# Page numbers read ahead, three fill banks in the attention, and two passes of the last block moved into the linear attention

## What is computed

```python
def compress_blocks(rows, pe, w1, w2):            # rows: all tokens' K or V, past pages included
    blk = rows[:, :nb * 64].reshape(B, nb, 64, 2, G, D)
    h = jax.nn.silu(jnp.einsum('bnlcgd,lcde->bncge', blk + pe[:, :, None, :], w1))
    return jnp.einsum('bncge,cef->bncgf', h, w2)

def nsa(x, ...):                                  # prompt and sample group alike
    q, q_rot, cmp_kv, slc_kv, win_kv, gates = nsa_project(x, pos, w_in, b_gate)
    o_cmp, imp = cmp_attention(q, pos, compress_blocks(...))
    o_slc = sel_attention(q_rot, ..., select_blocks(imp, pos, nb_sel), slc_kv)
    o_win = win_attention(q_rot, ..., win_kv)
    return (gates[0] * o_cmp + gates[1] * o_slc + gates[2] * o_win) @ w_out

def gla(x, s0, ...):                              # chunks of 32 tokens
    o = att @ v + q_i @ S;  S = a_last * S + k_s.T @ v
    return (rms_norm(o) * norm_g * silu(r)) @ w_out

y = layer_norm(ALPHA * y + mixer(y));  y = layer_norm(ALPHA * y + swiglu(y))
```

## Time and profile before

| | |
|---|---|
| time, median of 3 runs | 1784.22 us (1784.01 to 1786.27) |
| the profiled execution: its own time | 1787.92 us |
| its span, first to last instruction | 1786.2 us |
| TensorE matmul busy | 1644.1 us, 92% |
| TensorE weight load busy | 1496.4 us, 84% |
| DVE, ACT, POOL busy | 595.9, 577.5, 722.5 us |
| mean granted TensorE clock | 0.954 |
| phase_compress | about 177 to 325 us |
| attention, stretch with `keys` and `scores` | about 350 to 489 us |
| phase_gla ends, t1 begins | 1331.65 us |

### The profile page before, as it was taken

The page is one execution under the profiler, slowest core; times in us unless marked ns, Lnnn a source line. Parts: engine busy times, 40 slices in busy tenths (PEclk is TensorE's granted clock), DMA queues, the critical chain, the costliest instruction groups (busy, mean ns, idle before and its releaser), DMA issues. The chain is left out here.

```text
span 1786.2 us, 37763 instructions
## 1 busy us (share of the span) xinstructions
PE 1644.1 (92%) x14970; PEld 1496.4 (84%) x14970; DVE 595.9 (33%) x1212; ACT 577.5 (32%) x1142; POOL 722.5 (40%) x503
## 2 busy tenths in 40 slices
PE   6998789688989978999999998998979999999997
PEld 6998677465666678999999998987659999999996
DVE  2111010545555638211111138127547411111114
ACT  3221000255454525422322224226434532222313
POOL 6640321343344556644344327403126644334320
PEclk9998898699999989999999999999979999999998
DMA  7326885254535643433333213324214233323201
GB/s 209 104 81 164 253 269 183 74 160 145 156 113 173 180 130 118 144 116 118 108 117 93 85 48 95 86 70 144 81 60 130 86 116 95 89 86 99 86 22 48
DMA packets 297287, 211.56 MB, mean 118 GB/s; under 512 B 34148, under 2 KB 290328, under 8 KB 296600
## 3 DMA queue, kind: packets, MB, share of 16 engines
q1 hardware_dynamic: 279000, 175.69, 33.1%
q0 software_dynamic: 7552, 20.06, 3.6%
q10 hardware_dynamic: 10560, 13.41, 2.7%
HBM read 199.02 MB, written 18.42 MB: 122 GB/s over the span
## 5 line engine op out<-in xcount | busy, mean ns | idle before, releaser
L1582 POOL TENSOR_TENSOR w_low_t<-w_raw,w_high_t 128x1024 fp32r<-128x1024 f32 (+1 forms) x130 | 307.0, 2370 | 336.8 <-ACT w_high_t L1685 336.8
L1665 PE MATMUL ps<-x_high,w_high_t 128*128 128x256 f32 (+1 forms) x1488 | 425.4, 286 | 8.3 <-POOL w_low_t L1582 5.9
L1667 PE MATMUL ps<-x_high,w_low_t 128*128 128x256 f32 (+1 forms) x1488 | 421.6, 283 | 0.0
L1666 PE MATMUL ps<-x_low,w_high_t 128*128 128x256 f32 (+1 forms) x1488 | 420.9, 283 | 0.0
L1665 PEld LDWEIGHTS ps<-x_high,w_high_t 128*128 128x128 f32 x1488 | 281.9, 189 | 10.6 <-POOL w_low_t L1582 6.2
L1666 PEld LDWEIGHTS ps<-x_low,w_high_t 128*128 128x128 f32 x1488 | 282.2, 190 | 0.3
L1667 PEld LDWEIGHTS ps<-x_high,w_low_t 128*128 128x128 f32 x1488 | 282.1, 190 | 0.0
L1685 ACT CAST w_high_t<-w_raw 128x1024 fp32r<-128x1024 f32 (+1 forms) x130 | 132.0, 1024 | 154.3 <-PE ps L1667 126.1
L1807 DVE TENSOR_TENSOR h_t<-silu_t,ps 128x256 f32<-128x256 f32 (+1 forms) x88 | 37.4, 425 | 366.2 <-PE ps L1667 359.7
L1665 PE MATMUL ps<-hid_high,w_high_t 128*128 128x264 f32 (+1 forms) x542 | 153.6, 283 | 0.0
L1667 PE MATMUL ps<-hid_high,w_low_t 128*128 128x264 f32 (+1 forms) x542 | 153.2, 283 | 0.0
(11 more groups left out here) (367 smaller groups left out, 3208.2 us busy)
## 6 DMA issues: line engine op xcount, KB each, us to landing
w_raw<-in_ffn_w_gu SPq DMA_DIRECT2D x88, 512.0 KB, 3.8
pages<-in_cache_slc SPq DMA_DIRECT2D x192, 128.0 KB
rows<-in_cache_cmp SPq DMA_DIRECT2D x123, 128.0 KB, 3.7
w_raw<-in_ffn_w_down SPq DMA_DIRECT2D x32, 448.0 KB, 3.5
w_raw<-in_gla_w_in SPq DMA_DIRECT2D x24, 512.0 KB, 3.8
rows<-in_cache_cmp ACTq DMA_DIRECT2D x70, 128.0 KB, 4.9
pages<-in_cache_slc POOLq DMA_DIRECT2D x64, 128.0 KB, 2.8
w_raw<-in_ffn_w_down SPq DMA_DIRECT2D x16, 512.0 KB, 3.7
```

Of the source, the lines that this page charges most:

```text
L1582: nc.gpsimd.tensor_tensor(low(u)[:, 0:k], raw[:, u % RAW, 0:k], high(u)[:, 0:k].bitcast(F32), ALU.subtract).then_inc(low_done, 1)
L1665: nc.tensor.matmul(psum(i), high(u)[:, k, :], a[0][:, at, c], start=(k == 0), stop=False)
L1666: nc.tensor.matmul(psum(i), high(u)[:, k, :], a[1][:, at, c], start=False, stop=False)
L1667: ins = nc.tensor.matmul(psum(i), low(u)[:, k, :], a[0][:, at, c], start=False, stop=(k == t.kc - 1))
```

## The change

Three edits, without a change to what is computed or to the number of matmuls, copies or transfers.

1. **Page numbers.** A helper `row_pages` reads a queue's page numbers of a unit; the numbers of unit 1 are read in phase_project (SP: ahead of issuing the new caches; ACT: behind the `w1` loads; GpSimd: at its end). In phase_compress `load_part` only waits and issues, and `read_ahead` reads the numbers of the next unit behind it. ACT's `load_part` for unit n+2 now stands ahead of the sigmoid of unit n, with the wait for the buffer. SP's nine tables move behind the loads of unit 2 (six) and unit 3 (three). The two loads of position rows now stand behind GpSimd's reads for unit 5.
2. **Fill banks.** In the first part of the attention (the first 182 of the 366 steps, 116 of the 190 fills) the fills go round three banks, 4, 6 and 5. The outputs of `pv` move to columns 384 to 511 of bank 7, beside the sample scores. A `pv` of an even unit waits until DVE has taken all scores before it (`sc_out`), a `scores` step until DVE has taken out all finished pairs (`o_done`), and DVE takes a pair out at the next `qk` or `scores` step. `scores` steps that fell between an even `pv` and its odd one are moved behind the odd one: 8 of 20 move, and some groups of `keys` with them. From step 182 on all is as before.
3. **Passes.** The first two passes of t1 (units 0 and 1, tokens 0 to 255) are made inside phase_gla, one behind the last `kv`, one behind the last `o`, in banks 2 and 3, which `kv` has left. t1 begins with its third pass.

```diff
+def row_pages(eng, S, n, by):
+    p = n % (NB * PAGES // ROW_UNIT)
+    return [eng.value_load(S["pt"][0:1, p * ROW_UNIT + m:p * ROW_UNIT + m + 1], min_val=0, max_val=N_POOL - 1)
+            for m in range(ROW_SHARE[by], ROW_SHARE[by + 1])]
...
             for m in range(LATE):
                 first_page(sp, m)
+            S["next_pages"][0] = row_pages(sp, S, 1, 0)
...
         def load_part(eng, n, by, arrived):
-            c, p = UN[n]
-            lo, hi = SHARE[by], SHARE[by + 1]
-            pages = [eng.value_load(pt[0:1, p * QP + m:p * QP + m + 1], min_val=0, max_val=N_POOL - 1)
-                     for m in range(lo, hi)]
             if n >= 2:
                 eng.wait_ge(conv_done, n - 1)
-            for m, page in zip(range(lo, hi), pages):
+            for m, page in zip(range(SHARE[by], SHARE[by + 1]), S["next_pages"][by]):
...
+        def read_ahead(eng, n, by):
+            if n < len(UN):
+                S["next_pages"][by] = row_pages(eng, S, n, by)
...
         def _(pool):
             for n, (c, p) in enumerate(UN):
                 if n:
                     load_part(pool, n, 2, rows_sw)
+                    read_ahead(pool, n + 1, 2)
                 if n and p == 0:
...
         def _(act):
+            load_part(act, 1, 1, rows_act)
             for c in range(2):
                 act.dma_start(w2[64 * c:64 * c + 64], io["nsa_w_cmp2"][0, c]).then_inc(w2_in, 16)
-            load_part(act, 1, 1, rows_act)
+            read_ahead(act, 2, 1)
...
+                if n + 2 < len(UN):
+                    load_part(act, n + 2, 1, rows_act)
                 act.wait_ge(pre_done, n + 1)
                 if n >= 1:
                     act.wait_ge(hid_done, n)
                 nc.scalar.activation(sig[own, :, 0:k], pre[own, :, 0:k], ACT.Sigmoid).then_inc(sig_done, 1)
-                if n + 2 < len(UN):
-                    load_part(act, n + 2, 1, rows_act)
+                read_ahead(act, n + 3, 1)
...
+    dealt, ORDER, held, pair_open = ORDER, [], [], False
+    for step in dealt:
+        if step[0] == "scores" and pair_open or held and step[0] == "keys" and step[1] >= held[0][1] + 2:
+            held.append(step)
+            continue
+        ORDER.append(step)
+        if step[0] == "pv":
+            pair_open = UN[step[1]][2] == 0
+            if not pair_open:
+                ORDER += held
+                held = []
...
+    SLOT = [f % 3 if f < FILLS3 else (f - FILLS3) % 2 for f in range(len(FILL))]
+    TURN_OF = [SLOT[0:f + 1].count(SLOT[f]) for f in range(len(FILL))]
...
-        SCORE, OUT, SAMPLE = (0, 2), 5, 7
-        BANK = (4, 6)
+        SCORE, SAMPLE = (0, 2), 7
+        BANK = (4, 6, 5)
+        def out_of(n):
+            return ps[:, SAMPLE, 384:384 + P] if n in NEAR else ps[:, BANK[2], 0:P]
...
+                if n in NEAR:
+                    pe.wait_ge(own_masked, 1)
+                    if SCORES_TO["pv", n, 0]:
+                        pe.wait_ge(sc_out, SCORES_TO["pv", n, 0])
+                elif ORDER[SWITCH] == ("pv", n, 0):
+                    pe.wait_ge(fill_out[2], SLOT.count(2))
...
+                if PAIRS_TO["scores", i, 0]:
+                    pe.wait_ge(o_done, PAIRS_TO["scores", i, 0])
...
         def psum(i):
-            return ps[:, i % STAT, 0:width(passes[i][1])]
+            return ps[:, (i + begun) % STAT, 0:width(passes[i][1])]
...
+                if i < begun:
+                    continue
...
         ORDER.append(("kv", 2 * t + 1))
+        if t == TILES - 1:
+            ORDER.append(("next", 0))
...
+    ORDER.append(("next", 1))
     ORDER += [("rec", TILES - 1), ("norm", TILES - 1), ("oT", TILES - 1), ("gate", TILES - 1)]
...
+            def next_pass(u):
+                pe.wait_ge(cst["pre_low"]["t1"], u + 1)
+                pe.wait_ge(xh_done, 2)
+                pe.wait_ge(xl_done, 3)
+                pe.wait_ge(st_done, 8 * (len(KV) - 1) + 2 * (u + 1))
...
+                ins.then_inc(cst["pre_mm"], 1)
```

More of the change, by code:

```diff
@@ L934, in phase_attention @@
     ORDER += [x[:3] for x in sample[at_s:]]
-    FILL = {step: f for f, step in enumerate(x for x in ORDER if x[0] in ("turn", "keys", "probs", "back"))}
+    dealt, ORDER, held, pair_open = ORDER, [], [], False
[9 more added lines that the diff above has]
+                held = []
+    FILL = {step: f for f, step in enumerate(x for x in ORDER if x[0] in ("turn", "keys", "probs", "back"))}
+    LAST_SCORES = max(at for at, x in enumerate(ORDER) if x[0] == "scores")
+    SWITCH = next(at for at, x in enumerate(ORDER) if at > LAST_SCORES and x[0] == "pv" and UN[x[1]][2] == 0)
+    NEAR = {x[1] for at, x in enumerate(ORDER) if at < SWITCH and x[0] == "pv"}
+    FILLS3 = sum(x in FILL for x in ORDER[0:SWITCH])
+    SLOT = [f % 3 if f < FILLS3 else (f - FILLS3) % 2 for f in range(len(FILL))]
+    TURN_OF = [SLOT[0:f + 1].count(SLOT[f]) for f in range(len(FILL))]
+    SCORES_TO = {x: sum(y[0] == "scores" for y in ORDER[0:at]) for at, x in enumerate(ORDER) if x[0] == "pv"}
+    PAIRS_TO = {x: sum(y[0] == "pv" and UN[y[1]][2] == 1 for y in ORDER[0:at])
+                for at, x in enumerate(ORDER) if x[0] == "scores"}
+    WHOLE_AT = {}
+    for at, x in enumerate(ORDER):
+        if x[0] == "pv" and UN[x[1]][2] == 1:
+            WHOLE_AT[next(y for y in ORDER[at:] if y[0] in ("qk", "scores"))] = x[1]
     def by_act(step):
@@ L963, in phase_attention @@
                              "scaled4", "pv_done4", "o_done4"))
-        fill_done, fill_out = sem("fill_done"), [sem("fill_out%d" % b) for b in range(2)]
+        fill_done, fill_out = sem("fill_done"), [sem("fill_out%d" % b) for b in range(3)]
         ring = S["ring"]
@@ L1077, in pv @@
                     for a in range(2):
-                        nc.tensor.matmul(ps[own(a), OUT, 0:P], S["vb"][:, split_heads(p, a), :], S["pT"][:, t, :],
+                        nc.tensor.matmul(out[own(a)], S["vb"][:, split_heads(p, a), :], S["pT"][:, t, :],
                                          start=True, stop=False, tile_position=(0, 64 * a))
@@ L1083, in pv @@
                         c = (2 * (p // R) + a) * D
-                        ins = nc.tensor.matmul(ps[own(a), OUT, 0:P], v[:, k, c:c + D], pT[:, n % 2, a * (t + 1) + k, :],
+                        ins = nc.tensor.matmul(out[own(a)], v[:, k, c:c + D], pT[:, n % 2, a * (t + 1) + k, :],
                                                start=False, stop=(br == 1 and k == t), tile_position=(0, 64 * a))
@@ L1363, in _ @@
                 kind, n, f = step
-                if kind == "qk" and n > VLAG and UN[n - VLAG - 1][2] == 1:
-                    out_whole(n - VLAG - 1)
+                if step in WHOLE_AT:
+                    out_whole(WHOLE_AT[step])
                 if kind == "qk" and n < U:
@@ L1458, in load_unit, with phase_trunk @@
         sp.dma_start(raw[:, u % RAW, 0:t.kc], t.W[:, t.k0:t.k0 + t.kc, t.col:t.col + P]).then_inc(w_in[u % RAW], 16)
-def phase_trunk(nc, io, ps, cst, name, xT, X, H, stages, bounds, store, early=0, cast=0, moved=None, then=None):
+def phase_trunk(nc, io, ps, cst, name, xT, X, H, stages, bounds, store, early=0, cast=0, begun=0, moved=None, then=None):
     walk = Walk(stages, bounds)
@@ L1648, in _ @@
                     turn((i - first_half - 3) // 2)
-                if hf == 0:
+                if i < begun:
+                    continue
+                if hf == 0 or (u, 0) in passes[0:begun]:
                     split(pe, u)
@@ L2235, in turn_sample @@
                 ins.then_inc(fill_done, 1)
+            def next_pass(u):
[3 more added lines that the diff above has]
+                pe.wait_ge(st_done, 8 * (len(KV) - 1) + 2 * (u + 1))
+                c = slice(*SPLIT[0])
+                out = ps[:, BEGUN + u, 0:c.stop]
+                for kk in range(KT):
+                    nc.tensor.matmul(out, cst["w_high"][:, u, kk, :], X[0][:, kk, c], start=(kk == 0), stop=False)
+                    nc.tensor.matmul(out, cst["w_high"][:, u, kk, :], X[1][:, kk, c], start=False, stop=False)
+                    ins = nc.tensor.matmul(out, cst["w_low"][:, u, kk, :], X[0][:, kk, c], start=False, stop=(kk == KT - 1))
+                ins.then_inc(cst["pre_mm"], 1)
             for kind, n in ORDER:
@@ L2239, in _ @@
                     project(n)
+                elif kind == "next":
+                    next_pass(n)
                 elif kind == "low":
```

63 lines of the change are left out of this document (39 added, 24 removed).

## The result

The changed kernel takes 1774.1 us (median of 4 runs, 1770.45 to 1775.33), the one before 1784.95 us beside it (4 runs, 1784.01 to 1786.27): a ratio of 0.9936, 95% interval 0.9924 to 0.9949, or 10.9 us less. The forecast was 1771, 13.2 less. Of the three terms behind it one came out at less than half, one at two to three times its size.

A forecast was written before the change was run, and what follows sets the result against it. TensorE was taken to wait for late pages in phase_compress, bank copies in the attention and a chain ending phase_gla. Terms -10.4 - 2.3 - 0.5 = -13.2 us, from 1784.22 to 1771 us; range 1758 to 1779.

The forecast's parts named there:

- Rival A: phase_compress: transfers are the bound, later gaps stay, unit 1 gains 6.8, unit 4 pays 2.3; total 1777 us, chance 0.16.
- Edit 1, -10.4 forecast: phase_compress: pages issued earlier shrink the gaps ahead of units to 9.5 us, 10.4 us faster; ends -16 and -2.
- Pages are there at 194.3 instead of 201.09: phase_compress, unit 1: 4.2 MB at 317 GB/s take 13.2 us from 181.1, leaving a gap of 2.2 of 9.03 us.
- The covers: Reads for unit 1 in phase_project cost nothing, up to 7.5 us otherwise; DVE's product behind ACT's sigmoid is due a unit later.
- The cost of unit 4: phase_compress: position rows issued behind nine reads land last, so a gap of 2.3 us stands where 1.96 was.
- Edit 2, -2.3 forecast: Attention's keys stretch: third bank gains 10.5 us, new stalls cost 8.2, so 2.3 us faster; ends -11 and +3.
- The sum of the cost: Attention: nine scores waits of 0.8 us, 7.2, plus 1 us for even pv waits: 8.2 us.
- of 12.0 us I leave 1.5: Attention: a third bank covers TensorE's bank waits of up to about 1.2 us, a gain of 10.5 us.
- Rival B: Attention: the stalls cost nothing since DVE empties banks meanwhile, gain 10.5 us; total 1763, chance 0.22.
- Rivals C and D: Attention: C, third bank gives nothing, +3, total 1776, chance 0.13; D, bank 7 waits, +22.6, total 1807, chance 0.04.
- Edit 3, -0.5 forecast: End of phase_gla and t1's start: t1 begins 1.6 us later, its first pass ends 0.5 us earlier; ends -2.5 and +2.
- next 0: phase_gla: t1's first pass made ahead, behind the last kv, from about 1312.3 to 1317.0 at the low clock.

The follow-up runs named there:

- f1: The changed kernel, with ACT's and GpSimd's queues issuing unit 2's pages only when SP's pages of unit 1 have landed: 1771.39 us, ratio 0.9926.
- e2: The kernel before with edit 2 (fill banks) alone: 1778.70 us, ratio 0.9972 to the kernel before.
- e1: The kernel before with edit 1 (page numbers) alone: 1781.12 us, ratio 0.9975 to the kernel before.
- e3: The kernel before with edit 3 (passes) alone: 1785.28 us, ratio 1.0002 to the kernel before.
- g0: The changed kernel timed once more, nothing altered: 1774.66 us, ratio 0.9939 to the kernel before.
- e4: The changed kernel with its fills in two banks (4, 6) throughout, bank 7 and moved scores kept: 1786.97 us, ratio 1.0016 to the kernel before.
- f3: The changed kernel with each scores step at least one step behind an odd pv: 1771.68 us, ratio 0.9927 to the kernel before.
- g2: The changed kernel with cache writes behind SP's pages of unit 1, position rows ahead of GpSimd's reads, and scores a step later: 1770.07 us, ratio 0.9912.
- g3: The changed kernel with the edits of g1 and g2 together: 1769.49 us, ratio 0.9917 to the kernel before.
- g1: The changed kernel with only one pass of t1 made in phase_gla, behind the last o: 1772.32 us, ratio 0.9922 to the kernel before.

## Why the prediction was right and wrong

**The total** (1771 against 1774.1, inside the range of 1758 to 1779, "faster" at 0.93) was right by two errors of opposite sign. Each of the two was of some 3 to 6 us, so it was luck that the total came within some 3 us. Rival A's -4.5 us for phase_compress was met in number, but it was 6.8 gained at unit 1 and 2.3 lost at unit 4, where the traces have 3.9 at unit 1 and about 1 behind it; what A said of the later gaps, that they stay, holds but for this 1 us. Its total of 1777 was missed, for edit 2's sake. Of the readings named in advance, unit 1 came at 197.13 for 194 and unit 7 at 293.19 for 290, though the phase began 3.1 us early; waits for `kTs` came at 3.5 us (2.3 and 1.2) for under 2, and waits for a pair at 5.1 for 7.

**Edit 1, -10.4 forecast, -4.5 timed.** Two steps failed.

- The reading that was to prove it wrong, a gap near 9 us ahead of unit 1, came out (8.1). "Pages are there at 194.3 instead of 201.09" gave 4.2 MB the engines to themselves until the last byte. They were issued 3 us earlier than reckoned, but the compress weights held the engines until 178, so the reckoned start of the transfers was about right. Unit 1 yet began at 197.1 to 197.2 in three of the four executions whose phase begins near 174.4, and at 199.95 in the fourth, for which no run gives a cause. Unit 2's pages are issued when unit 0 ends and take 1.55 of the 2.7 MB that still move. f1, which holds them back, puts their price at 1.9 us; the other 1.0 us beyond 194.3 is the tail of SP's queue, which moves 0.10 MB in 2.2 us with nothing beside it. That unit 0's end starts the next load stood in the account of `conv_done`; it wasn't applied to unit 1. The gain is 3.9 us where 6.8 stood.
- For the later units the state after the change was right (7.2 us of gaps, 7.3 forecast), but the 10.9 before were taken from one execution, and another of the same code (e2) has 7.4. Of 3.6 us forecast 1.3 are there in the means, and the ranges overlap.
- The covers held: reads in phase_project cost nothing (the phase begins at 174.38 in e1 as in e2 and e3), and no row shows a unit waiting on ACT's later sigmoid. The cost of unit 4 was right in kind: the position rows were last to land (e1), with 1.5 us where 2.3 stood.

The Trainium skill, "DMA: Bandwidth & Descriptors", section "Issuing engines are not separate DMA queues", says that queues share the same engines, so that spreading issue saves sequencer time only. The prediction set it aside since reading and issuing took longer than a page's transfer. The trace agrees with the rule once the next unit's pages are in the queues: they interleave with SP's last pages, and without them unit 1 starts 1.9 us earlier (f1). For the rest the time ahead of the issue did count: edit 1, which takes reads and tables out of it, saved 4.5 us.

**Edit 2, -2.3 forecast, -5.0 timed and -5.8 to -6.7 in the stretch (e2, the change and g0 against before, e1 and e3).** The sum of the cost was right, 7.8 us with two banks for 8.2, its parts less so: the nine waits for a pair were 0.5 to 0.6 us each for 0.8, and 1.8 us for `nmx` weren't in it. The failed step is the gain: "of 12.0 us I leave 1.5" read the waits alone. The third bank brought 14.4 us, 4.9 of them waits that the profile counts as busy. Rival B (stalls cost nothing, gain 10.5) is not borne out: with two banks bank 7 and the moved steps cost 7.8 us (e4), and with three 3 us of them cost 1.1 to 1.6 (f3, g2, g3). Rivals C and D fell with the first reading, no `scores` of the change having waited more than 0.85 us for a pair.

**Edit 3, -0.5 forecast, 0.0 timed (to within 1.6 us), -0.3 by the traces' means.** Its size is below what the times can tell. Each step came out in the rows: next 0 took 4.3 us at a low clock that rose within it (0.50 until 1299, then 0.99; 4.7 us forecast), `o` began 2.6 us later (2.8) and took 4.7 (4.8), and t1's weights were made 1.3 us later (1.6). g1 hints at what the loss of cover costs: with one pass left in t1 the same edit gives 0.8 us more by the means of the traces, which is not clear of their scatter.

## What to carry to other kernels

Before a gap of the profiled execution is counted as gain, look whether its start is fixed by an engine or by the transfers behind it: compare absolute starts, and remember that one execution's gaps can be 3 us off. When waits on a buffer are many and short, those listed are a lower bound; what a further buffer is worth shows in the length of the stretch, not in its idle time. Work moved ahead of a barrier may have been the cover of what comes behind it (10.05 us of waiting at t1's start where there were 6.27): look first how much fits into a wait that is there.
